# LayerNorm's power on GpSimd for both tiles at once, conv taps dealt anew, a gate moved ahead of the retention scalings

## What is computed

```python
x = x + 0.5 * swiglu_ffn(rmsnorm(x), ...)                 # FFN 1
q, k, v, g, p, c, gates = split(rmsnorm(x) @ w_in)
y_ret  = (retention(q, k, v) * silu(g)) @ w_ret_out       # 4 heads, two chunks of 128 tokens
y_pool = pool_mixer(p, w_pool, pool_scale)
# conv branch:
u = a * sigmoid(b)                                        # a, b = split(c), 512 channels
y = causal depthwise conv of u, 31 taps, + conv_b
y = silu(layernorm(y, ln_g, ln_b)); y_conv = y @ w_conv_out
x = x + (sig(g_ret) * y_ret + sig(g_pool) * y_pool + sig(g_conv) * y_conv) @ w_out
x = x + 0.5 * swiglu_ffn(rmsnorm(x), ...)                 # FFN 2
```

## Time and profile before

| | |
|---|---|
| median of 3 runs | 1195.56 us (1194.2 to 1196.89) |
| the profiled execution | 1197.01 us, its span 1194.9 us |
| TensorE busy | 1173.4 us (98%), 5374 matmuls |
| VectorE busy | 753.5 us (63%) |
| ScalarE busy | 540.8 us (45%) |
| GpSimd busy | 52.8 us (4%) |
| mean transfer rate | 184 GB/s |
| chain that ended last | TensorE 89%, VectorE 9%, issue 2% |

### The profile page before, as it was taken

How to read it: one execution, slowest core, us unless ns; L and a number is a source line. 1 busy time by engine, 2 the same in 40 slices (tenths; PEclk the granted TensorE clock), 3 DMA queues, 4 the chain that set the end, 5 groups by cost and what they waited for, 6 DMA issues and landing times.

```text
span 1194.9 us, 13340 instructions
## 1 busy us (share of the span) xinstructions
PE 1173.4 (98%) x5374; PEld 968.0 (81%) x5374; DVE 753.5 (63%) x906; ACT 540.8 (45%) x599; POOL 52.8 (4%) x81
## 2 busy tenths in 40 slices
PE   8999999999998999999999999999999989999997
PEld 6888888888787888888888888888887878888886
DVE  6555365798996655444465545367979967554542
ACT  7444335453534554434364444354434445444332
POOL 2000001000102010000010000010000011000000
PEclk9999999999998999999999999999999999999999
DMA  9744464553553545535564545555336634554440
GB/s 363 277 158 188 148 242 171 196 185 111 211 193 129 191 174 199 190 129 214 207 240 156 204 152 209 182 196 206 126 115 228 224 142 170 200 207 155 167 176 36
DMA packets 33805, 220.02 MB, mean 184 GB/s; under 512 B 3776, under 2 KB 4160, under 8 KB 8912
## 3 DMA queue, kind: packets, MB, share of 16 engines
q1 hardware_dynamic: 31248, 212.09, 48.3%
q0 software_dynamic: 1648, 6.06, 1.5%
q10 hardware_dynamic: 848, 1.02, 0.2%
HBM read 218.11 MB, written 1.05 MB: 183 GB/s over the span
## 4 chain that ended last, share of the span: by engine, by line
PE 89%; DVE 9%; issue 2%; ACT 0%; DMA 0%; POOLq 0%; POOL 0%; DVEq 0%; ACTq 0%
PE acc L321 28%; PE acc L323 28%; PE acc L322 28%; PE tr L381 4%; DVE y L1136 4%; DVE w_lo L948 3%; DVE gates L1156 1%; DVE gates L1204 0%; DVE ua L1185 0%; PE tr L473 0%; DMA ident_gain<-in_ident 0%; PE tr L483 0%; DVE qk L1194 0%; DVE qk L1212 0%; DVE sideT_lo L1162 0%
## 5 line engine op out<-in xcount | busy, mean ns | idle before, releaser
L948 DVE TENSOR_TENSOR w_lo<-raw,w_hi 128x2048 fp32r<-128x2048 f32 (+1 forms) x206 | 448.5, 2213 | 101.2 <-ACT w_hi L633 100.6
L633 ACT CAST w_hi<-raw 128x2048 fp32r<-128x2048 f32 (+1 forms) x206 | 378.8, 1851 | 289.3 <-PE acc L323 288.6
L321 PE MATMUL acc<-w_hi,xT_hi 128*128 128x512 f32 x1184 | 473.7, 400 | 1.1 <-DVE w_lo L958 1.1
L323 PE MATMUL acc<-w_hi,xT_lo 128*128 128x512 f32 x1184 | 464.3, 392 | 0.0
L322 PE MATMUL acc<-w_lo,xT_hi 128*128 128x512 f32 x1184 | 463.3, 391 | 0.0
L323 PEld LDWEIGHTS acc<-w_hi,xT_lo 128*128 128x128 f32 x1184 | 223.5, 189 | 48.3
L321 PEld LDWEIGHTS acc<-w_hi,xT_hi 128*128 128x128 f32 x1184 | 224.2, 189 | 45.2 <-DVE w_lo L958 1.0
L322 PEld LDWEIGHTS acc<-w_lo,xT_hi 128*128 128x128 f32 x1184 | 224.3, 189 | 43.4
L1003 DVE SCALAR_TENSOR_TENSOR h<-acc,rs,silu_gate 128x256 f32<-128x256 f32 x88 | 42.6, 484 | 219.4 <-ACT silu_gate L682 219.4
L321 PE MATMUL acc<-w_hi,hT_hi 128*128 128x512 f32 x352 | 137.9, 392 | 0.0
L323 PE MATMUL acc<-w_hi,hT_lo 128*128 128x512 f32 x352 | 137.1, 389 | 0.0
(11 more groups left out here) (118 smaller groups left out, 574.2 us busy)
## 6 DMA issues: line engine op xcount, KB each, us to landing
raw<-in_weights SPq DMA_DIRECT2D x194, 1024.0 KB, 4.8
raw<-in_weights SPq DMA_DIRECT2D x10, 512.0 KB, 3.7
bias<-in_gate_bias POOLq DMA_DIRECT2D x6, 512.0 KB, 5.2
raw<-in_weights SPq DMA_DIRECT2D x8, 256.0 KB, 3.8
scale_row<-in_pool_scale POOLq DMA_DIRECT2D x2, 512.0 KB, 10.0
x<-in_x SPq DMA_DIRECT2D x3, 256.0 KB, 7.8
band<-in_band POOLq DMA_DIRECT2D x1, 768.0 KB, 6.5
decay<-in_decay POOLq DMA_DIRECT2D x1, 512.0 KB, 5.2
```

The source lines that it names most:

```text
L321: nc.tensor.matmul(o, a_hi, b_hi, start=first, stop=False)
L323: return nc.tensor.matmul(o, a_lo, b_hi, start=False, stop=last)
L633: nc.scalar.copy(w_hi[:, hf % HIGHS, 0:n], raw[:, hf % RAWS, 0:n]).then_inc(hi_split, 1)
L948: nc.vector.tensor_tensor(w_lo[:, hf % RAWS, 0:n], raw[:, hf % RAWS, 0:n], w_hi[:, hf % HIGHS, 0:n].bitcast(F32), ALU.subtract).then_inc(l ...
```

## The change

On GpSimd the eight LayerNorm instructions of a layer become one, a power on both tiles' variances (128x2). VectorE adds EPS for both tiles (`ln_eps`) after the statistics, does the gate that it did there before, and then the negated product (`ln_shifts`) when the power is done. ScalarE's `ln_apply` waits for that one. VectorE's 124 taps are dealt out anew: 81 in place of 66 ahead of `gate_z(l, POOLED, 1, 0)`, and 43 in place of 58 behind it. `gate_z(l, POOLED, 1, 1)` and the four `merge_first` come ahead of `retained`, with the two subtractions of `subs(M_POOL)` between the merges. `gate_z(l, RET, 0, 0)` comes ahead of the first `side_low` of the retention. TensorE transposes the retention's output later, after slice 6 of M_GATE_RET's tile 0 and slice 1 of tile 1.

```diff
--- before.py
+++ after.py
@@ -139,8 +139,8 @@
         head_rs = sb("head_rs", [P, T, HEADS])
         ln_stats = sb("ln_stats", [P, T, 6])
         ln_mean_var = sb("ln_mean_var", [P, T, 2])
-        ln_small = sb("ln_small", [P, 4, T])
-        ln_var, ln_rstd, ln_minus, ln_shift = (ln_small[:, i, :] for i in range(4))
+        ln_small = sb("ln_small", [P, 3, T])
+        ln_var, ln_rstd, ln_shift = (ln_small[:, i, :] for i in range(3))
 
 
 
@@ -233,7 +233,6 @@
         ln_mean_ready = sem("ln_mean_ready")
         ln_var_ready = sem("ln_var_ready")
         ln_rstd_ready = sem("ln_rstd_ready")
-        ln_negated = sem("ln_negated")
         ln_shift_ready = sem("ln_shift_ready")
         constants_set = sem("constants_set")
         setup_dve = sem("setup_dve")
@@ -536,9 +535,8 @@
                                                      5: lambda: inner(l, 3)})
                 in_block(l, M_GATE_POOL + 1, 1)
                 pool_product(l)
-                in_block(l, M_GATE_RET, 0, mid={3: lambda: turn_ret(l, 0),
-                                                6: lambda: turn_ret(l, 1)})
-                in_block(l, M_GATE_RET, 1)
+                in_block(l, M_GATE_RET, 0, mid={6: lambda: turn_ret(l, 0)})
+                in_block(l, M_GATE_RET, 1, mid={1: lambda: turn_ret(l, 1)})
                 in_block(l, M_GATE_RET + 1, 0)
                 in_block(l, M_GATE_RET + 1, 1)
                 for t in range(T):
@@ -770,7 +768,7 @@
 
             def ln_apply(l, t):
                 name = ("y", l, t)
-                act.wait_ge(ln_shift_ready, l * T + t + 1)
+                act.wait_ge(ln_shift_ready, l + 1)
                 nc.scalar.activation(pin[:, t, :], bank(name), ACT.Identity,
                                      bias=ln_shift[:, t:t + 1], scale=ln_rstd[:, t:t + 1]
                                      ).then_inc(tr_taken[TURN[name] % 2], 1)
@@ -936,7 +934,7 @@
         @block.vector
         def _(dve):
             nc.vector.memset(scale_row[:, 0:NB // 2], 0.0).then_inc(warm_set, 1)
-            for i, value in enumerate((-0.5, EPS, 0.5, 1.0 / DH, -1.0)):
+            for i, value in enumerate((-0.5, EPS, 0.5, 1.0 / DH)):
                 nc.vector.memset(small[:, i:i + 1], value).then_inc(constants_set, 1)
             x_high_count = [0]
 
@@ -1231,6 +1229,16 @@
                 nc.vector.bn_aggr(ln_mean_var[:, t, :], ln_stats[:, t, :]
                                   ).then_inc(ln_mean_ready, 1)
 
+            def ln_eps(l):
+                dve.wait_ge(ln_mean_ready, l * T + T)
+                nc.vector.tensor_scalar(ln_var, ln_mean_var[:, :, 1], EPS, None, ALU.add
+                                        ).then_inc(ln_var_ready, 1)
+
+            def ln_shifts(l):
+                dve.wait_ge(ln_rstd_ready, l + 1)
+                nc.vector.scalar_tensor_tensor(ln_shift, ln_mean_var[:, :, 0], -1.0, ln_rstd,
+                                               ALU.mult, ALU.mult).then_inc(ln_shift_ready, 1)
+
             def conv_low(l, i):
                 s = (slice(None), slice(2 * i, 2 * i + 2), slice(None))
                 dve.wait_ge(side_hi_ready, l * 6 + 4 + i + 1)
@@ -1267,50 +1275,54 @@
 
                 rotary(l, 1, 1)
                 subs(M_V)
-                conv_taps(l, 14)
+                conv_taps(l, 15)
 
                 subs(M_G)
-                conv_taps(l, 16)
+                conv_taps(l, 17)
 
                 subs(M_P)
                 scale_pool(l, 0)
-                conv_taps(l, 16)
+                conv_taps(l, 18)
 
                 decayed(l, 0)
                 decayed(l, 1)
                 scale_pool(l, 1)
                 subs(M_GATE_POOL)
+                conv_taps(l, 8)
                 side_low(l, ("pooled", l, 0), (slice(None), slice(0, 2), slice(None)), 2, 1)
                 gate_z(l, POOLED, 0, 0)
+                conv_taps(l, 3)
                 side_low(l, ("pooled", l, 1), (slice(None), slice(2, 4), slice(None)), 2, 2)
-                conv_taps(l, 10)
+                conv_taps(l, 4)
 
                 decayed(l, 2)
                 decayed(l, 3)
                 gate_z(l, POOLED, 0, 1)
                 subs(M_GATE_POOL + 1)
+                conv_taps(l, 6)
                 gate_z(l, POOLED, 1, 0)
-                conv_taps(l, 16)
+                conv_taps(l, 9)
+
+                gate_z(l, POOLED, 1, 1)
+                merge_first(l, 0, 0)
+                sub(l * HALVES + 2 * M_POOL + 3)
+                merge_first(l, 1, 0)
+                merge_first(l, 0, 1)
+                sub(l * HALVES + 2 * M_POOL + 4)
+                merge_first(l, 1, 1)
+
                 retained(l, 0)
                 retained(l, 1)
-
-                gate_z(l, POOLED, 1, 1)
-                merge_first(l, 0, 0)
-                merge_first(l, 1, 0)
-                merge_first(l, 0, 1)
-                merge_first(l, 1, 1)
-                subs(M_POOL)
-
                 subs(M_GATE_RET)
+                gate_z(l, RET, 0, 0)
                 side_low(l, ("ret", l, 0), (slice(None), slice(None), tokens(0)), HEADS, 3)
-                gate_z(l, RET, 0, 0)
+                conv_taps(l, 8)
                 side_low(l, ("ret", l, 1), (slice(None), slice(None), tokens(1)), HEADS, 4)
-                conv_taps(l, 14)
 
                 gate_z(l, RET, 0, 1)
                 subs(M_GATE_RET + 1)
                 gate_z(l, RET, 1, 0)
-                conv_taps(l, 14)
+                conv_taps(l, 12)
 
                 gate_z(l, RET, 1, 1)
                 subs(M_RET)
@@ -1327,7 +1339,9 @@
                 for t in range(T):
                     ln_stat(l, t)
                     ln_mean(l, t)
+                ln_eps(l)
                 gate_z(l, CONV, 0, 1)
+                ln_shifts(l)
                 subs(M_GATE_CONV + 1)
                 gate_z(l, CONV, 1, 0)
                 for i in (0, 1):
@@ -1376,7 +1390,7 @@
 
         @block.gpsimd
         def _(pool):
-            pool.wait_ge(constants_set, 5)
+            pool.wait_ge(constants_set, 4)
 
             def norm_factor(l, norm):
                 for t in range(T):
@@ -1430,20 +1444,9 @@
                 wait_gates_done(l, RET)
                 load_bias(l, CONV)
 
-                for t in range(T):
-                    pool.wait_ge(ln_mean_ready, l * T + t + 1)
-                    nc.gpsimd.tensor_tensor(ln_var[:, t:t + 1], ln_mean_var[:, t, 1:2],
-                                            small[:, 1:2], ALU.add).then_inc(ln_var_ready, 1)
-                    pool.wait_ge(ln_var_ready, l * T + t + 1)
-                    nc.gpsimd.tensor_tensor(ln_rstd[:, t:t + 1], ln_var[:, t:t + 1],
-                                            small[:, 0:1], ALU.pow).then_inc(ln_rstd_ready, 1)
-                    nc.gpsimd.tensor_tensor(ln_minus[:, t:t + 1], ln_mean_var[:, t, 0:1],
-                                            small[:, 4:5], ALU.mult).then_inc(ln_negated, 1)
-                    pool.wait_ge(ln_rstd_ready, l * T + t + 1)
-                    pool.wait_ge(ln_negated, l * T + t + 1)
-                    nc.gpsimd.tensor_tensor(ln_shift[:, t:t + 1], ln_minus[:, t:t + 1],
-                                            ln_rstd[:, t:t + 1], ALU.mult
-                                            ).then_inc(ln_shift_ready, 1)
+                pool.wait_ge(ln_var_ready, l + 1)
+                nc.gpsimd.tensor_tensor(ln_rstd, ln_var, small[:, 0:1].broadcast_to([P, T]),
+                                        ALU.pow).then_inc(ln_rstd_ready, 1)
 
             for l in range(L):
                 norm_factor(l, 0)
```

## The result

The changed kernel takes **1179.3 us** (median of 4 runs, 1179.19 to 1179.75) against 1195.65 us (1194.2 to 1196.89) for the kernel before: a ratio of 0.9862, interval 0.985 to 0.9874, or 16.4 us less. 1178.2 us was forecast, with a range of 1174 to 1183.5.

What follows compares the result with a forecast made beforehand. TensorE was taken to bound the kernel, losing time at two waits per layer and to the slow clock behind them. 20.8 us removed less 3.5 us added gave 17.4 us off 1195.56: 1178.2 us, range 1174 to 1183.5.

Steps and rivals of the forecast that it cites:

- The bound: TensorE, busy 98% of the span; two waits per layer, in pool_product (2.46 us) and at turn_yn (3.65 us), plus slow clock.
- Change 1: Pooled gate ahead of retained: the 2.46 us wait in pool_product and its slow stretch go, 4.17 us a layer.
- The new wait: At turn_ret(l, 0), TensorE waiting for the scalings of retained: about 1.3 us a layer, 2.6 us in two.
- rival (a): The clock falls after the wait at turn_ret, costing 1.7 us a layer: 1181.6 us; chance 0.17.
- the first gain: The pool_product wait and its slow stretch removed by the pooled gate ahead of retained: 8.3 us in two layers.
- Change 2: 15 more taps ahead of gate_z(POOLED, 1, 0), 6.0 us hidden in DVE's 8.8 us idle time; last tap ends at 352.8.
- Rival (c): DVE's idle time doesn't take the taps in full; TensorE waits 1.1 us at turn_yn, clock loss up to 1.7: 1183.8; chance 0.08.
- Change 3: LayerNorm with one GpSimd power of two elements: the turn_yn wait and slow stretches go, 11.9 us in two layers.
- The worst case: LayerNorm's GpSimd power held like the old one, 2.48 us: ready 0.2 us too late for turn_yn.
- The new wait before M_CONV: TensorE reaches M_CONV sooner than conv_low: 0.46 us, 0.9 us in two layers, less 0.2 that layer 1 has now.
- The sum: 20.8 us removed, 3.5 us added, net 17.4 us less, taken from the runs' median of 1195.56 us: 1178.2 us.
- the slow stretch after the second wait: Behind the turn_yn wait: clock 0.51 over 6.2 us and 0.69 over 5.1 us, 3.04 and 1.58 us of work lost.

Runs made afterwards that it cites:

- G alone: Kernel before with only the pooled gate and merges ahead of the scalings of retained and turn_ret later; taps and LayerNorm as before: 1196.37 us, ratio 1.0003.
- L and T: Changed kernel with gate, merges and turn_ret put back to their old places, leaving the LayerNorm part and the new deal of taps: 1177.68 us, ratio 0.985.
- L alone: Kernel before with only the LayerNorm part (one GpSimd power, ln_eps and ln_shifts on VectorE): 1185.51 us, ratio 0.9913.
- L and G: Changed kernel with the old deal of the taps, leaving the LayerNorm part and the moved gate, merges and turn_ret: 1185.8 us, ratio 0.9918.
- T alone: Kernel before with only the new deal of the taps, the gate staying behind retained: 1181.42 us, ratio 0.9877.
- G and T: Changed kernel with the old GpSimd LayerNorm chain, keeping the moved gate, merges and turn_ret and the new deal of taps: 1183.95 us, ratio 0.9899.

## Why the prediction was right, point by point

**The bound.** That only TensorE's two waits and their slow stretches could be won back held: with both gone, the span fell by what the list of waits and the clock rows had said.

**Change 1.** The gate was forecast for 307.25 and ran there; `retained` was to be ready at 315.95 and TensorE went on at 315.93. The new wait was to be 1.26 us (315.95 less 314.69) and was 1.45 less 0.23, that is 1.22 us. (Two of the prediction's sums are off by under 0.1 us: 308.0 + 2.39 + 4.40 + 1.03 is 315.82 and not 315.85, and 186 x 0.227 is 42.2 and not 42.3.) Its clock price was taken as nothing, from the row of the kernel's start, and was nothing; rival (a), with 0.17, did not come. But the prediction booked the first gain, 8.3 us, to the move of the gate. G alone gave nothing, and L and T without it gave more than with it. The gain belongs to the 15 taps: they let the gate come in time, and they let VectorE end its taps before TensorE wants them, without which even a clock that stays up brings nothing (L alone). The sum was right since it priced the whole, and since it said that the taps were needed to keep the first gain. One more working, with 9 taps and the scalings ahead of the gate (306.09 + 2.07 = 308.2, its bank wanted at 309.20), would have shown that the move isn't needed.

**Change 2.** The 15 taps were to be hidden in VectorE's gaps. They were: `decayed` came 0.9 us later (1.2 forecast), TensorE's retention products began at 281.17 as in the earlier trace rows, and the gate at 301.79 as in the earlier trace rows. The last tap was to end at 352.8 and did so at 352.7 (350.26 + 2.46); TensorE came to `turn_y` at 354.36, forecast 354.2. Rival (c) did not come.

**Change 3.** The power for two elements was to take 0.73 us, by the line between 0.56 and 1.77, and took 0.72. `turn_yn` found both `ln_apply` done: they ended at 362.26 and were wanted at 364.15, 1.9 us in hand where 1.4 were forecast. The worst case, a power held like the old one, was to miss by 0.2 us (0.3 by its own terms); with a subtraction beside the power (2.69 us) TensorE lost 0.44 us. The reason given, that no subtraction stands between power and `ln_shifts`, is shown by the two kernels with one put there. The reading of the Trainium skill ("GPSIMD Engine Reference", Key points) came out in halves. A subtraction, with two SBUF inputs, holds the power (2.69 us), and the gate, with one, doesn't. But that the eight-element power in the earlier trace rows had been held by the taps, which have two as well, is not borne out: 0.56, 0.72 and 1.77 us for one, two and eight elements lie on one line within 0.1 us, though the last ran beside taps. Here the rows differ from what the prediction made of that section of the Trainium skill, and the rows decide. The new wait before M_CONV was to be 0.46 us and was 0.36 (0.59 from start to start, less 0.23): the chain took 4.68 us (4.6 forecast), and TensorE's own work 4.32 (4.13 forecast).

**The sum.** 17.4 us were forecast. The two profiled executions differ by 17.8 us (1197.01 and 1179.24) and their spans by 17.5. The medians differ by 16.4. So **the step that was off is the subtraction of a sum made on one execution from the median of others**: the profiled execution of before is 1.4 us above its median. Beside the changed kernel on another chip, where seven executions of the kernel before were all near that one (1196.13 to 1197.02 us, median 1196.58), the difference was 17.2 us. The record points at the slow clock: of the 20 executions of before on the chip where the parts were measured, the five with a mean granted clock of 0.996 or 0.997 took 1194.0 to 1195.0 us, and the 15 with 0.992 to 0.994 took 1195.2 to 1197.1. The term of the sum that can carry this is the slow stretch after the second wait, 3.04 us in layer 0 and 1.58 in layer 1 for waits of equal length. G alone keeps both waits at the LayerNorm, 3.48 and 3.47 us idle, and its profiled execution, at 1195.75 us, has 0.75 over 6.3 us and 0.79 over 8.0 us behind them: 1.6 and 1.7 us lost. So a stretch of 3.04 us is not the rule. The kernel before and G alone scatter by 3 us on that chip, the two with 2.0 and 2.4 us of wait (`ln_shifts` behind the subtractions, the longer wait) by 1.7 and 1.9, and all others by 0.3 to 0.9. That the missing 1 us lies in this stretch and not in another is an inference; no profile of a shorter execution of the kernel before was taken.

## What to carry to other kernels

Follow the late instruction's queue back on its own engine and count what stands ahead of it: here it was seven taps and not the scalings, and filling earlier gaps of VectorE with work that has no due time gave 14.4 us alone, while the move that looks like the cure gave nothing. Price a change's parts alone and together: a wait of the engine that bounds the kernel hides how late the next engine is, and two parts can shorten the same wait, so their gains don't add up. And keep long VectorE instructions with two SBUF inputs from running beside a GpSimd step that is waited for (2.69 us in place of 0.72), and from standing in VectorE's queue ahead of the step that waits for it (6.2 us here).

## What the runs showed of the hardware

- **The same wait can cost the clock or not.** Idle times of TensorE of 1.07, 1.48, 1.93 and 1.98 us left the clock at 1.00. 2.01 us brought it down in layer 0 of one kernel, and 2.02 us in its layer 1 did not; 2.06 us did in layer 1 of G alone and not in its layer 0, and did in both layers of L and G; 2.30 us did in both layers of before and 2.29 us in neither of L alone. 2.43 us (the longer wait at `turn_ret`) and 3.47 to 3.49 us (before and G alone) did it each time. All are of the profiled executions. The two layers of G alone:

```profile
317.00:323.00 6.00, 5.53 (x28) 4.65 (x29) 6.00 (x9) 2.05 (x3) 0.00 (x0) 1.00 0.17 69
906.00:912.00 6.00, 5.44 (x21) 4.58 (x22) 6.00 (x9) 1.17 (x2) 0.00 (x0) 0.72 0.21 87
```

The expectations for T alone and for G and T put a slow stretch behind waits of 2.1 to 2.2 us; the waits were 1.5 and 2.0 and no stretch came. That is most of their miss of 3.4 and 3.5 us.
- **A 128x2048 subtraction on VectorE holds a GpSimd power that begins beside it until it ends** (2.69 us in place of 0.72); a 128x512 gate with one operand in PSUM doesn't (0.72 us).
